# A hybrid decoder step: x transposed behind each landing, and gate/up weights in pieces of eight rows

## What is computed

```python
h = rmsnorm(x, g_mix); p = h @ w_in            # 2048 -> 3072: conv value | conv gate | pool input
yc = silu(layernorm(depthwise_conv31(v * sigmoid(gate))))
yp = (trailing_means_2_4_8_16(u) - u) @ w_pool * pool_scale
x = x + concat(yc, yp) @ w_out
h = rmsnorm(x, g_ffn)                          # top-1 of 4 groups, top-2 of its 8 experts
for e in range(32):
    y += gates[:, e] * ((silu(h @ w_gate[e]) * (h @ w_up[e])) @ w_down[e])
out = rmsnorm(x + y, g_final)
```

## Time and profile before

| | us |
|---|---|
| median of 3 runs | 1410.45 (1408.94 to 1411.17) |
| the profiled execution, own time | 1409.55 |
| its span | 1407.8 |
| PE busy | 1250.1 (89%) |
| DVE busy | 344.2 (24%) |
| ACT busy | 121.3 (9%) |
| POOL busy | 116.5 (8%) |
| moved by DMA | 464.61 MB, mean 330 GB/s |

### The profile page before, as it was taken

How to read it: one execution, slowest core, us unless ns; L and a number is a source line. 1 busy time by engine, 2 the same in 40 slices (tenths; PEclk the granted TensorE clock), 3 DMA queues, 4 the chain that set the end, 5 groups by cost and what they waited for, 6 DMA issues and landing times.

```text
span 1407.8 us, 16671 instructions
## 1 busy us (share of the span) xinstructions
PE 1250.1 (89%) x6515; PEld 711.9 (51%) x6515; DVE 344.2 (24%) x677; ACT 121.3 (9%) x242; POOL 116.5 (8%) x166
## 2 busy tenths in 40 slices
PE   8999989999999999989988898998898998898850
PEld 7777767777875444444333443433344343344210
DVE  4299953011251110110101011010111101011017
ACT  1100013000100000000000000000000000000003
POOL 2211143000000000000000000000000000000004
PEclk9999999999999999999999999999999999999985
DMA  8533423566349999999999999999999999999964
GB/s 233 163 120 119 153 86 107 198 247 243 133 190 373 421 423 426 423 422 421 424 423 423 424 421 423 422 423 424 422 423 422 424 421 424 420 423 419 379 193 124
DMA packets 100790, 464.61 MB, mean 330 GB/s; under 512 B 10095, under 2 KB 52207, under 8 KB 62115
## 3 DMA queue, kind: packets, MB, share of 16 engines
q1 hardware_dynamic: 95088, 455.89, 81.1%
q0 software_dynamic: 5392, 7.86, 1.8%
q10 hardware_dynamic: 283, 0.48, 0.1%
HBM read 456.67 MB, written 20.80 MB: 339 GB/s over the span
## 4 chain that ended last, share of the span: by engine, by line
DMA 50%; PE 35%; issue 7%; DVE 6%; SPq 1%; ACT 0%; ACTq 0%; DVEq 0%; POOLq 0%
DMA arena<-in_w_up_dram 48%; PE bank L546 13%; PE bank L699 13%; PE bank L718 3%; DVE arena L931 3%; PE bank L678 2%; PE bank L494 1%; DMA arena<-expert_rows 1%; SPq L381 1%; DMA pv<-in_pool_scale_dram 1%; PE bank L613 1%; DVE arena L1179 1%; DVE tn L891 0%; PE bank L583 0%; PE bank L630 0%
## 5 line engine op out<-in xcount | busy, mean ns | idle before, releaser
L699 PE MATMUL bank<-arena,stage 128*64 128x512 f32 x1920 | 429.4, 595 | 74.3 <-DMA arena<-in_w_up_dram 74.3
L699 PEld LDWEIGHTS bank<-arena,stage 128*64 128x64 f32 x1920 | 139.4, 137 | 356.7 <-issue 293.4
L546 PE MATMUL bank<-arena,stage 128*128 128x288 f32 x1280 | 315.0, 407 | 0.8 <-DVE arena L914 0.8
L546 PEld LDWEIGHTS bank<-arena,stage 128*128 128x128 f32 x1280 | 241.9, 190 | 66.3 <-issue 0.9
L678 PEld LDWEIGHTS bank<-x1w,x1r 96*128 96x128 f32 x1536 | 174.0, 192 | 26.0 <-issue 26.0
L678 PE MATMUL bank<-x1w,x1r 96*128 96x128 f32 x1536 | 180.2, 277 | 0.0
L1150 DVE TENSOR_TENSOR a_sb<-sl_sb,bank 128x256 f32<-128x256 f32 x32 | 19.4, 606 | 504.8 <-ACT sl_sb L843 504.8
L718 PE MATMUL bank<-arena,aT 128*64 128x512 f32 x512 | 113.4, 595 | 8.5 <-ACT aT L845 8.5
L1292 POOL DMA_INDIRECT expert_rows<-ysb,cur_d x32 | 31.3, 978 | 882.1 <-DVE ysb L1159 880.7
L931 DVE SCALAR_TENSOR_TENSOR arena<-arena,wdw 128x256 f32<-128x256 f32 x240 | 103.0, 501 | 0.0
L1159 DVE COPY ysb<-bank 128x512 f32<-128x512 f32 x32 | 22.1, 691 | 261.3 <-PE bank L718 261.3
(11 more groups left out here) (212 smaller groups left out, 494.2 us busy)
## 6 DMA issues: line engine op xcount, KB each, us to landing
arena<-in_w_gate_dram SPq DMA_DIRECT2D x112, 1024.0 KB, 17.0
arena<-in_w_up_dram SPq DMA_DIRECT2D x112, 1024.0 KB, 25.5
arena<-in_w_down_dram SPq DMA_DIRECT2D x30, 2048.0 KB, 21.5
xT<-in_w_down_dram SPq DMA_DIRECT2D x15, 2048.0 KB, 24.1
stage<-in_w_down_dram SPq DMA_DIRECT2D x15, 2048.0 KB, 25.5
stage<-in_w_in_dram SPq DMA_DIRECT2D x11, 2048.0 KB, 8.3
stage<-in_w_out_dram SPq DMA_DIRECT2D x8, 2048.0 KB, 8.1
stage<-in_w_gate_dram SPq DMA_DIRECT2D x16, 512.0 KB
```

Of the source, the lines that this page charges most:

```text
L546: last = pe.matmul(ps[bank][:, 0:NTOK], wsl[a][:, k, cc * P:(cc + 1) * P], rhs[:, k, :], start=(n == 0), stop=(n == KT - 1))
L699: last = pe.matmul(ps[4 + s][BLK * h:BLK * (h + 1), :], xgT[:, k, BLK * s:BLK * (s + 1)], w[:, :, 256 * h:256 * (h + 1)], start=(k == 0), ...
```

## The change

It does three things. The transpose of `pv` on PE moves behind the transposes of all three tiles of x, and ACT's copy of it behind ACT's root of the variance. The unread products fall from 12, 10, 8 and 20 to 12, 7, 6 and 10. And the buffer of the gate and up weights has two pieces of eight rows in place of four of four rows: a DMA brings eight rows of gate or of up (2 MB; 1.5 MB for piece 0 of the second expert of a pair), there are two semaphores `gu_in`, PE waits before groups 0 and 8 alone, and SP waits until two of the four counts of `gu_used` have come before it reloads a piece. Between the slices of `w_out`, each of the four slots takes one such DMA.

```diff
--- before.py
+++ after.py
@@ -40,8 +40,8 @@
 NBLK = 2 * (PAIRS + OVP)
 PAD = 4096
 
-AWAKE_START = (12, 10, 8)
-AWAKE_SCALE = 20
+AWAKE_START = (12, 7, 6)
+AWAKE_SCALE = 10
 HISTB = (4, 6, 7, 5, 4, 6)
 AWAKE_ROUTE = (40, 18)
 SELB = (0, 1, 7, 0)
@@ -216,7 +216,7 @@
         ak = words(arena, O_AK, CT * AK).rearrange("p (j t) -> p j t", j=CT)
         uk = words(arena, O_UK, CT * UK).rearrange("p (j t) -> p j t", j=CT)
         strow = words(arena, O_HT, 2 * DC, AK).rearrange("p (a c) -> p a c", a=2)
-        wgu = words(arena, 0, GU_WORDS).rearrange("p (c g k f) -> p c g k f", c=4, g=2, k=4)
+        wgu = words(arena, 0, GU_WORDS).rearrange("p (c g k f) -> p c g k f", c=2, g=2, k=8)
 
         wdn = [[words(arena, GU_WORDS + 2 * h * D, 2 * D) for h in range(2)],
                [words(xT, 0, 2 * D), words(stage, 2 * D, 2 * D)]]
@@ -252,7 +252,7 @@
         half_in = sem("half_in")
         slot_in = [sem(f"slot_in{a}") for a in range(2)]
         first_in = sem("first_in")
-        gu_in = [sem(f"gu_in{c}") for c in range(4)]
+        gu_in = [sem(f"gu_in{c}") for c in range(2)]
         wd_in = [[sem(f"wd_in{s}{h}") for h in range(2)] for s in range(2)]
 
         st_out = sem("st_out")
@@ -374,11 +374,10 @@
             sp.wait_ge(u_mm, 6)
             sp.dma_start(wsl[0][:, 0:CT, :], wpool).then_inc(slot_in[0], 16)
 
-            def load_gu(e, c, s=0):
-                k = 2 if s == 1 and c == 0 else 4 * c
-                for g, src in ((0, wgate), (1, wup)):
-                    w = src[:, bass.DynSlice(e, 1), k:4 * c + 4, :].rearrange("p o k f -> p (o k f)")
-                    sp.dma_start(wgu[:, c, g, k - 4 * c:4, :].rearrange("p k f -> p (k f)"), w).then_inc(gu_in[c], 16)
+            def load_gu(e, c, g, s=0):
+                k = 2 if s == 1 and c == 0 else 8 * c
+                w = (wgate, wup)[g][:, bass.DynSlice(e, 1), k:8 * c + 8, :].rearrange("p o k f -> p (o k f)")
+                sp.dma_start(wgu[:, c, g, k - 8 * c:8, :].rearrange("p k f -> p (k f)"), w).then_inc(gu_in[c], 16)
 
             def load_first(e):
                 for g, src in ((0, wgate), (1, wup)):
@@ -406,7 +405,7 @@
                     sp.wait_ge(st_out, 16 * 4)
                     sp.wait_ge(old_out, 16 * 2)
                 if c in (1, 3, 4, 5):
-                    load_gu(0, (1, 3, 4, 5).index(c))
+                    load_gu(0, *((0, 0), (0, 1), (1, 0), (1, 1))[(1, 3, 4, 5).index(c)])
                 if c == 6:
                     sp.wait_ge(mix_ready, CT)
                     load_wd_part(0, 0, 1, 1)
@@ -426,9 +425,10 @@
 
 
             def gate_up(e, n, s):
-                for c in range(4):
-                    sp.wait_ge(gu_used, 4 * n + c - 3)
-                    load_gu(e, c, s)
+                for c in range(2):
+                    sp.wait_ge(gu_used, 4 * n + 2 * c - 2)
+                    for g in range(2):
+                        load_gu(e, c, g, s)
 
             def first_gate_up(e, n):
                 sp.wait_ge(gu_used, 4 * n - 7)
@@ -504,9 +504,8 @@
                     for k in range(4 * b, 4 * b + 4):
                         last = pe.transpose(ps[b][:, (k % 4) * TR:(k % 4 + 1) * TR], x1r[:, t, k * P:(k + 1) * P], ident[0:TR, 0:TR])
                     last.then_inc(xT_mm, 1)
-                if t == 0:
-                    pe.wait_ge(pv_in, 16 * 6)
-                    pe.transpose(ps[7][:, 0:64], pv[:, :], ident[0:64, 0:64]).then_inc(pvT_mm, 1)
+            pe.wait_ge(pv_in, 16 * 6)
+            pe.transpose(ps[7][:, 0:64], pv[:, :], ident[0:64, 0:64]).then_inc(pvT_mm, 1)
 
             stay_awake(AWAKE_SCALE, 6)
             pe.wait_ge(diag_ready, 1)
@@ -690,11 +689,12 @@
                                 select(0, b)
                         if s == 0:
                             pe.wait_ge(xgT_ready, 4 * i + c + 1)
-                        pe.wait_ge(gu_in[c], 32 * n + 32)
+                        if c % 2 == 0:
+                            pe.wait_ge(gu_in[c // 2], 32 * n + 32)
                         if s == 1 and c == 0:
                             pe.wait_ge(first_in, 32 * i + 32)
                         for k in range(4 * c, 4 * c + 4):
-                            w = wgu_first[:, :, k, :] if s == 1 and k < 2 else wgu[:, c, :, k - 4 * c, :]
+                            w = wgu_first[:, :, k, :] if s == 1 and k < 2 else wgu[:, k // 8, :, k % 8, :]
                             for h in range(2):
                                 last = pe.matmul(ps[4 + s][BLK * h:BLK * (h + 1), :], xgT[:, k, BLK * s:BLK * (s + 1)],
                                                  w[:, :, 256 * h:256 * (h + 1)], start=(k == 0), stop=(k == KT - 1))
@@ -752,11 +752,10 @@
                     act.wait_ge(xT_mm, 4 * t + b + 1)
                     act.copy(xTk[:, 4 * b:4 * b + 4, t * TR:(t + 1) * TR],
                              ps[b][:, 0:4 * TR].rearrange("p (k t) -> p k t", k=4)).then_inc(xT_ready, 1)
-                if t == 0:
-                    act.wait_ge(pvT_mm, 1)
-                    act.copy(pvT[:, :], ps[7][:, 0:64]).then_inc(pvT_ready, 1)
             act.wait_ge(act_in, 1)
             act.activation(sq[:, :], va[:, :], ACT.Sqrt).then_inc(sqrt_done, 1)
+            act.wait_ge(pvT_mm, 1)
+            act.copy(pvT[:, :], ps[7][:, 0:64]).then_inc(pvT_ready, 1)
 
             def values(g):
                 for cc in range(2):
```

## The result

The changed kernel takes 1397.03 us (1395.81 to 1399.46, 4 runs) where the kernel before takes 1410.23 (1408.94 to 1411.17, 4 runs): a ratio of 0.9916, with a 95% interval of 0.9904 to 0.9927. The profiled execution after took 1395.81 us with a span of 1394.0, 13.8 less than the span before.

What follows compares the result with a forecast made beforehand. The prediction took the expert part to run at the pace of its weight loads by DMA; terms -8.2 + 0 + 1.9 + 3.5 = -2.8 us gave 1407.6 us from the median, range 1402 to 1413.

Steps and rivals of the forecast that it cites:

- The start: Term 1, the kernel's start: without PE's 3.88 us stand for the small vectors, hT begins near 19.3, not 27.50: -8.2 us.
- the fall at 11.0: At the start before: granted clock falls to half at 11.0 us, so it had risen in the first block of transposes.
- The covers: At the start: both slices of w_in land before PE wants them, the first barely, so the earlier start isn't held up.
- The bytes of the stream: Term 2, the experts' weight loads: fewer, larger DMAs of the same bytes change nothing, 0, bounds +/-0.2 us an expert.
- a period other than 30.4: Expert part: a time per expert other than 30.4 us was named as a sign that the forecast is wrong.
- larger pieces do move faster: Rival on the weight stream: 0.05 us gained an issue, -6 us more, 1401.6 us; chance 0.10.
- The hole at the fill: Term 3, as the queue fills at expert 2: the later gate/up issue makes the stream 1.9 us late, bounds 0.5 and 3.6.
- Behind the last landing: Term 4, after expert 30's last piece lands: 32 products stand behind it instead of 16, +3.5 us.
- The clock at the waits: PE's joined waits of 2.9 us may drop its clock; 0 taken, rival +1.2 to +2.4 at the last wait, chance 0.22.
- The rival in which PE becomes the bound: Expert part: the clock falls in every expert and PE sets the pace, some +9 us, 1419 us; chance 0.10.
- The doubled wait: Expert part: PE's two waits of 1.5 and 1.4 us join to one of 2.9 us an expert.
- unchanged cover of 12 us: In the full weight queue, each gate/up piece is issued some 12 us before it is due, despite the coarser buffer waits.

Runs made afterwards that it cites:

- after_again: The changed kernel run once more, unchanged, as the measure for later runs on the same chip; 1397.2 us, 0.9908 of the kernel before.
- start_only: The kernel before with only the new start (vectors' transpose last, 12, 7, 6 and 10 unread products), weights in four-row pieces; 1403.61 us, 0.9953 of before.
- filled: The changed kernel with 8 unread products ahead of PE's wait for rows 8 to 15 of each expert but the first; 1398.71 us, 0.9923 of before.
- warm_less: The changed kernel without the 7, 6 and 10 unread products, keeping the 12 ahead of the first tile; 1401.81 us, 0.9947 of before.

## Why the prediction was wrong

- **The start, -8.2**: right. hT came 8.5 us earlier, the first gate/up product 8.7. The clock was at its high level from the first transposes on, as concluded from the fall at 11.0. The covers held. What was missed is how much the tiles' landings move between executions: hT stood at 18.98 after, at 19.14 in after_again and at 20.23 in start_only.
- **The bytes of the stream, 0**: this is the step that failed. The prediction said that two more issues and shorter lines cost -0.08 us, "nothing within what the rows resolve". It read this off two experts of different kinds, of which one loads `wgu_first` and the other not, and which differ in more than lines. It also gave the term a bound of 0.2 us an expert; 0.33 was measured. Its own sign of being wrong, a period other than 30.4, is what showed. The runs show 8.5 ns a line: 512 fewer lines are 0.27 us an expert, 7 of the 8.3 us; what is left, 0.06 us an expert, may be four issues fewer, the waits or the scatter between traces, and is not settled. By the same slope the kind with `load_first` should have had the longer period in the earlier trace rows by 0.14 us, and had one shorter by 0.08. That offset is not explained; a difference of two kinds could not carry the term.
- The rival "larger pieces do move faster" was the one that came true, with a chance of 0.10; it was put down to issues, at 6 us, and its time of 1401.6 lay outside the stated range. The Trainium skill has a figure that is nearer than the rule I weighed: in "DMA: Bandwidth & Descriptors", section "Bandwidth", a note on the floor of a 4 KB transfer issued from GpSimd puts about 10.5 ns on each packet. The page does not say it of long lines in a full queue. Carried over all the same, 32 lines an engine would be 0.34 us an expert, an estimate from that page; the slope measured here, 8.5 ns, gives 0.27. The rule that I did weigh, 2.0 us for each DMA, which the page too gives for DMAs issued from GpSimd, would be 8 us an expert and is not borne out.
- **The hole at the fill, +1.9**: something of it came, its size is not settled. The windows after:

```profile
435.00:438.00 3.00, 3.00 (x18) 1.00 (x16) 0.00 (x0) 0.00 (x0) 0.00 (x0) 1.00 0.97 365
438.00:441.00 3.00, 3.00 (x18) 1.00 (x16) 0.00 (x0) 0.00 (x0) 0.00 (x0) 1.00 1.00 365
441.00:444.00 3.00, 3.00 (x18) 0.99 (x14) 0.00 (x0) 0.00 (x0) 0.00 (x0) 1.00 1.00 426
...
524.00:526.00 2.00, 2.00 (x8) 0.80 (x6) 0.00 (x0) 0.00 (x0) 0.00 (x0) 0.52 1.11 473
```

  The issue for expert 2 came at 437.76, as worked out. At 365 GB/s for 6 us against 426, about 0.9 us of stream is missing, though the DMA engines are at a share of 0.97 and 1.00 there: a lower rate, not the idle hole of the forecast. Against it stand four experts' 0.33 us, and the table has -0.02 at expert 5. The other five traces with these lines and issues need 156.5 to 157.8 us from the first gate/up product to there, where it was 156.6 before and after. With 1.3 us for the four experts that makes a loss of 1.2 to 2.6 us, the forecast's 1.9 among them.
- **Behind the last landing, +3.5**: right, +3.24; PE's end is 39.0 us behind the landing where it was 35.6.
- **The clock at the waits**: it does fall at 11 of the 15 waits of 2.7 to 3.4 us (0.52 in the window of 524 to 526 above), at none of the shorter ones, and costs 1.5 to 3 us of PE each time, but no time in the period, since the next wait is shorter (some 0.7 us) or gone. The rival in which PE becomes the bound is refuted by filled. At the last landing it is paid or not: 7.09 us in the profiled execution after, 8.78 in after_again.
- The doubled wait, the unchanged cover of 12 us and the pace set by DMA were right. With 0.33 us for each of the 29 experts from 2 to 30 in place of 0, the terms give -8.7 + 0.9 - 9.6 + 3.2 = -14.2, against 13.8 less span; the 0.9 is the least certain of them.

## What to carry to other kernels

When a stage runs at the pace of its DMA queue, count the lines (one partition's run without a gap), not the DMAs: here 8.5 ns for each line on its engine, which makes 0.27 us of a period of 30.4, 0.9%, from 8 to 16 KB. To price such a thing from a trace, compare like with like over many periods, and let the bound of a term be multiplied by its count before calling it nothing. Unread products belong only inside a wait. There they cost nothing, and they win where PE's work behind the wait sets the time (4.6 us at this start), not where the next landing does (30.01 against 30.03 us an expert).

## What the runs showed of the hardware

- The rate of a full queue from DRAM depends on the line well above 4 KB: 415 GB/s with gate and up in 4 KB lines, 422 with 8 KB, 427 with 16 KB.
- Loads over 64 partitions with the same line of 16 KB let the 16 engines appear fully busy (a share of 1.01) and move 262 GB/s; the kernel took 2115.53 to 2196.89 us. Why was not tried further.
- The granted clock fell while PE was at work again, about a microsecond after a wait of 2.07 us had ended, in warm_less. No group behind the waits of up to 1.7 us in the expert part before is slowed (3.65 us for 16 products each time).
